# First loads by halves and quarters, constants behind the third unit, repeated bias tiles computed once, last norm spread over three engines

## What is computed

```python
def first_block(...):
    for layer in range(2):
        xn = rmsnorm(h, norm_mix[layer])
        # layer 0: q,k,v,p = xn @ ev_w_in; attention + causal pooling; @ ev_w_out
        # layer 1: gated projections, spatial gating, gated delta rule; @ od_w_out
        h = h + mix
        h = h + memory_cross_attention(rmsnorm(h, ...), mem_n, ...)
        h = h + conv_ffn(rmsnorm(h, ...), ...)
    return rmsnorm(h, final_norm)

def second_block(x, ..., rel_bias, norm_final_g):
    for i in range(2):
        # retention + nsa(...) from rms_norm(x) @ w_in[i], then a gated FFN
    return rms_norm(x, norm_final_g)
```

## Time and profile before

| | us |
|---|---|
| median of 3 runs | 2070.64 (2070.33 to 2073.42) |
| profiled execution, its own time | 2071.59 |
| its span, first to last instruction | 2069.7 |
| PE busy | 2012.6 (97%) |
| POOL busy | 1619.6 (78%) |
| ACT busy | 1085.4 (52%) |
| DVE busy | 866.5 (42%) |

### The profile page before, as it was taken

The page is one execution under the profiler, slowest core; times in us unless marked ns, Lnnn a source line. Parts: engine busy times, 40 slices in busy tenths (PEclk is TensorE's granted clock), DMA queues, the critical chain, the costliest instruction groups (busy, mean ns, idle before and its releaser), DMA issues.

```text
span 2069.7 us, 32431 instructions
## 1 busy us (share of the span) xinstructions
PE 2012.6 (97%) x12426; PEld 1754.1 (85%) x12426; DVE 866.5 (42%) x2030; ACT 1085.4 (52%) x2116; POOL 1619.6 (78%) x1291
## 2 busy tenths in 40 slices
PE   8999999999999999999999989999999999999997
PEld 7788999897888899898778858888997788678886
DVE  3422466066541466173323172563332412644641
ACT  3454566466245566445454585544444554865543
POOL 6495898977286798999799608899997897268997
PEclk9999999999999999999999999999999999999999
DMA  8653555553054476465446604555554467135553
GB/s 301 123 183 123 168 194 169 183 182 120 1 163 163 143 244 215 164 203 185 141 164 191 222 21 163 184 184 191 176 194 151 145 204 227 63 122 176 192 183 112
DMA packets 243470, 343.13 MB, mean 166 GB/s; under 512 B 8787, under 2 KB 171699, under 8 KB 243189
## 3 DMA queue, kind: packets, MB, share of 16 engines
q1 hardware_dynamic: 231320, 331.35, 48.7%
q10 hardware_dynamic: 11997, 9.72, 2.4%
HBM read 336.85 MB, written 4.19 MB: 165 GB/s over the span
## 4 chain that ended last, share of the span: by engine, by line
PE 83%; POOL 6%; DVE 3%; issue 3%; ACT 2%; DMA 1%; POOLq 1%; DVEq 0%; SPq 0%; ACTq 0%
PE bank L757 9%; PE bank L760 9%; PE bank L764 9%; PE bank L779 7%; PE bank L807 7%; PE bank L813 7%; PE bank L810 6%; POOL w_lo L1526 6%; PE bank L837 5%; PE bank L840 5%; PE bank L844 5%; PE bank L784 4%; DVE E L2197 1%; DVE E L2211 1%; DMA ring<-in_w_in 1%
## 5 line engine op out<-in xcount | busy, mean ns | idle before, releaser
L1526 POOL TENSOR_TENSOR w_lo<-ring,w_hi 128x512 fp32r<-128x512 f32 (+1 forms) x1216 | 1575.2, 1314 | 396.8 <-ACT w_hi L1617 359.7
L1617 ACT ACTIVATE w_hi<-ring 128x512 fp32r<-128x512 f32 (+1 forms) x1216 | 757.6, 630 | 791.0 <-PE bank L807 271.3
L757 PE MATMUL bank<-x_pair,w_hi 128*128 128x256 f32 x1504 | 381.6, 286 | 3.0 <-DVE x_pair L2112 2.3
L760 PE MATMUL bank<-x_pair,w_hi 128*128 128x256 f32 x1504 | 379.0, 284 | 0.0
L807 PE MATMUL bank<-w_hi,x_pair 128*128 128x512 f32 (+1 forms) x752 | 299.0, 398 | 2.9 <-issue 1.6
L757 PEld LDWEIGHTS bank<-x_pair,w_hi 128*128 128x128 f32 x1504 | 290.2, 193 | 5.9 <-ACT w_hi L1617 2.7
L810 PE MATMUL bank<-w_hi,x_pair 128*128 128x512 f32 (+1 forms) x752 | 292.9, 390 | 0.0
L760 PEld LDWEIGHTS bank<-x_pair,w_hi 128*128 128x128 f32 x1504 | 290.3, 193 | 0.4
L764 PE MATMUL bank<-x_pair,w_lo 128*128 128x256 f32 x1504 | 242.5, 284 | 0.0
L813 PE MATMUL bank<-w_lo,x_pair 128*128 128x512 f32 (+1 forms) x752 | 234.8, 394 | 4.2 <-POOL w_lo L1526 3.4
L764 PEld LDWEIGHTS bank<-x_pair,w_lo 128*128 128x128 f32 x1504 | 208.3, 193 | 0.0
(11 more groups left out here) (314 smaller groups left out, 2428.6 us busy)
## 6 DMA issues: line engine op xcount, KB each, us to landing
ring<-in_w_in SPq DMA_DIRECT2D x74, 1024.0 KB, 5.1
ring<-in_ffn_w_up SPq DMA_DIRECT2D x44, 1024.0 KB, 5.1
ring<-in_w_ffn_in SPq DMA_DIRECT2D x44, 1024.0 KB, 5.1
ring<-in_ffn_w_down SPq DMA_DIRECT2D x20, 1024.0 KB, 5.0
ring<-in_w_ffn_out SPq DMA_DIRECT2D x20, 1024.0 KB, 5.0
ring<-in_xattn_wkv SPq DMA_DIRECT2D x16, 1024.0 KB, 5.2
ring<-in_w_o_ret SPq DMA_DIRECT2D x16, 1024.0 KB, 5.0
ring<-in_od_w_in SPq DMA_DIRECT2D x12, 1024.0 KB, 5.1
```

What stands on the lines that cost most here:

```text
L757: m = mm(out_, view(w_hi)[:, k, :], x_hi[:, 4 * kh + k, :], start=start, stop=False)
L760: mm(out_, view(w_hi)[:, k, :], x_lo[:, 4 * kh + k, :], start=False, stop=False)
L1526: tt(view(w_lo), src, view(w_hi), ALU.subtract).then_inc(w_lo_ready, 1)
L1617: return A(o, i_, ACT.Copy, **kw)
```

## The change

Seven things, in the order of the program.

1. x is loaded as two halves by channels (`x_loads`, `x_second`), and the first half of eq as two quarters by columns (pieces 0 and 1, then 2 and 3). SP's order is now ident, x half 0, quarter 0, quarter 1, x half 1, eq half 1, ek, memory input, ev half 0, the tables, ev half 1, 16 constants, ep.
2. ACT issues one row load (norm_mix) ahead of its first work; the other 15 go between the rounding of ek's pieces, two behind each. The vector rows are transposed in the middle of ev, and DVE copies them out behind ek.
3. PE begins with 10 matmuls of zeros (`WARM`), 128x512, which wait for a DVE memset alone.
4. `cmpbias`: a bias depends on 128t - 16n only, so the tile (1, n+8) equals (0, n); PE makes 15 tiles, ACT copies 7 of them twice, and DVE fills the masked 8 with -1e30.
5. ACT loads the last gain ahead of the units `3down`.
6. In the last norm DVE takes statistics of columns 0 to 511 before it adds the second half; ACT squares and sums columns 512 to 1023; POOL multiplies columns 0 to 511 by the gain.
7. Once rstd is there, DVE finishes and SP stores columns 512 to 1023, ACT finishes and stores columns 0 to 511.

```diff
+CMP_SEEN = (P - CMP_LEN) // CMP_STRIDE + 1
+CMP_SHIFT = P // CMP_STRIDE
+CMP_TILES = [(0, n) for n in range(CMP_SEEN)] + [(1, n) for n in range(CMP_SHIFT)]
...
+        first_loads = units[0][1][0]
+        (whole_half, whole_source), = first_loads
+        first_weights, first_source = whole_half(0)[:, :, 0:2 * P], whole_source[:, :, 0:2 * P]
+        first_loads[0] = (lambda s: whole_half(s)[:, :, 2 * P:4 * P], whole_source[:, :, 2 * P:4 * P])
...
+            pe.wait_ge(nothing_ready, 1)
+            for _ in range(WARM):
+                mm(bank[0][:, :], nothing[:, 0:P], nothing[:, P:P + PIECE], start=True, stop=True)
             pe.wait_ge(ident_loaded, 16)
-            pe.wait_ge(first_rows, 48)
+            pe.wait_ge(first_rows, 16)
...
+            def turn_x():
+                pe.wait_ge(x_second, 16)
+                turn_h("0m", 1)
...
-            channel_major("eq", x_parts, key="0m", second_half=lambda: turn_h("0m", 1), before_last=turn_rows)
+            channel_major("eq", x_parts, key="0m", second_half=turn_x)
...
-            token_major("ev", x_parts)
+            token_major("ev", x_parts, after=turn_rows)
...
-            for t in range(TT):
-                for n in range(N_CMP):
+            for c, (t, n) in enumerate(CMP_TILES):
...
-            sp.dma_start(h[:, :, :], I["x"][0].rearrange("(t p) n -> p t n", p=P)).then_inc(x_loads, 16)
+            sp.dma_start(h[:, :, 0:512], x_src[:, :, 0:512]).then_inc(x_loads, 16)
+            sp.dma_start(first_weights, first_source).then_inc(first_quarter, 16)
...
             for n, (name, halves) in enumerate(units):
-                if n == 1:
+                if n == RING:
                     sp.dma_start(i_mem, ...).then_inc(mem_loads, 16)
-                if n == RING:
+                if n == RING + 1:
                     load_constants()
                 for j, loads in enumerate(halves):
+                    if n == 0 and j == 1:
+                        sp.dma_start(h[:, :, 512:D], x_src[:, :, 512:D]).then_inc(x_second, 16)
+                    if n == RING and j == 1:
+                        load_table()
...
+            pool.wait_ge(gain_loads, 32)
+            for t in range(TT):
+                B.wait_emptied(pool, ("3down", t, 0))
+                tt(xs[:, t, 0:512], h[:, t, 0:512], gain_row[:, 0:512], ALU.mult).then_inc(gained, 1)
             reciprocal_rms("out")
...
-            round_weights("ek")
+            for p in range(PIECES):
+                round_weights("ek", p, p + 1)
+                for dst, src in later_rows[2 * p:2 * p + 2]:
+                    act.dma_start(dst, src).then_inc(row_loads, 16)
...
+            for t in range(TT):
+                B.wait_emptied(act, ("3down", t, 1))
+                m = A(E[:, t, :], h[:, t, 512:D], ACT.Square, scale=D ** -0.5, accum_out=ms2[:, t:t + 1])
+            m.then_inc(final_square, 1)
+            act.wait_ge(gained, TT)
+            act.wait_ge(rstd_ready, RMS.index("out") + 1)
+            for t in range(TT):
+                copy(xs[:, t, 0:512], xs[:, t, 0:512], scale=rstd[:, t:t + 1]).then_inc(out_done, 1)
...
+                add_last(0)
+                for t in range(TT):
+                    nc.vector.bn_stats(h_stats[:, t, :], h[:, t, 0:512])
+                add_last(1)
+                for t in range(TT):
+                    nc.vector.bn_aggr(h_mv[:, t, :], h_stats[:, t:t + 1, :])
+                drain()
+                tt(ms[:, :], h_mv[:, :, 0], h_mv[:, :, 0], ALU.mult)
+                drain()
+                tt(ms[:, :], ms[:, :], h_mv[:, :, 1], ALU.add)
+                drain()
+                ts(ms[:, :], ms[:, :], 0.5, EPS, ALU.mult, ALU.add)
+                drain()
+                dve.wait_ge(final_square, 1)
+                tt(ms[:, :], ms[:, :], ms2[:, :], ALU.add).then_inc(ms_ready, 1)
...
-            dve.wait_ge(ident_loaded, 16)
+            nc.vector.memset(nothing[:, :].bitcast(F32), 0.0).then_inc(nothing_ready, 1)
+            nc.vector.memset(cmpbias[:, 0, CMP_SEEN:N_CMP, :].rearrange("p b c -> p (b c)"), -FAR)
```

More of the change, by code:

```diff
@@ L152 @@
 N_ROWS_PAD = -(-N_ROWS // P) * P
+EARLY_ROWS = ROWS["norm_mix"][1]
+assert ROWS["norm_mix"][0] == 0 and N_ROWS <= 512
 class Banks:
@@ L384, in build @@
         first_rows = sem("first_rows")
+        nothing_ready = sem("nothing_ready")
+        first_quarter = sem("first_quarter")
+        final_square = sem("final_square")
+        out_done = sem("out_done")
+        gained = sem("gained")
+        x_second = sem("x_second")
         row_loads = sem("row_loads")
@@ L1000, in turn_rows @@
                 B.take(pe, ("vec", 1), 2)
-                for r in range(1, N_ROWS_PAD // P):
+                for r in range(N_ROWS_PAD // P):
                     n = min(P, N_ROWS - r * P)
-                    m = tr(bank[2][:, (r - 1) * P:(r - 1) * P + n], i_rows[0:n, r, :], ident[0:n, 0:n])
+                    m = tr(bank[2][:, r * P:r * P + n], i_rows[0:n, r, :], ident[0:n, 0:n])
                 m.then_inc(full[2], 1)
@@ L1491, in _ @@
                         sp.dma_start(dst(n % RING), src).then_inc(landed[n % RING][j], 16)
[L1492 to L1495, removed]
+            for t in range(TT):
+                sp.wait_ge(h_done, t + 1)
+                sp.dma_start(out[0][t * P:(t + 1) * P, 512:D], xs[:, t, 512:D]).then_inc(stored, 16)
             sp.wait_ge(stored, 64)
@@ L1625, in round_weights @@
                 for p in range(first, end or pieces(name)):
-                    fresh = [j for j in halves_of(name, p) if j not in known]
-                    wait_landed(act, name, fresh)
-                    known.update(fresh)
+                    if name == "eq" and p < 2:
+                        act.wait_ge(first_quarter, 16)
+                    else:
+                        fresh = [j for j in halves_of(name, p) if j not in known]
+                        wait_landed(act, name, fresh)
+                        known.update(fresh)
                     if first_piece[name] or p >= HELD:
@@ L1720, in evacuate, with row_loads_of @@
                 A(dst, src, f, **kw).then_inc(empty[b], 1)
[L1723 to L1726, removed]
+            def row_loads_of(name):
+                r0, count = ROWS[name]
+                src, done = vector_rows(I[name]), 0
                 while done < count:
@@ L1729, in _ @@
                     k = min(count - done, P - r % P)
-                    act.dma_start(i_rows[r % P:r % P + k, r // P, :], src[done:done + k, :]).then_inc(first_rows if r < P else row_loads, 16)
-                    n += r >= P
+                    yield i_rows[r % P:r % P + k, r // P, :], src[done:done + k, :]
                     done += k
-            assert n == ROW_LOADS, n
+            later_rows = [load for name in ROWS if name != "norm_mix" for load in row_loads_of(name)]
+            assert len(later_rows) == ROW_LOADS
+            (dst, src), = row_loads_of("norm_mix")
+            act.dma_start(dst, src).then_inc(first_rows, 16)
             act.wait_ge(ident_loaded, 16)
@@ L2164, in finish, with add_last @@
             def finish():
-                for n in range(2):
+                dve.wait_ge(gain_loads, 32)
+                halves_ = [np.s_[:, t, n * 512:(n + 1) * 512] for n in range(2) for t in range(TT)]
+                def add_last(n):
                     for t in range(TT):
@@ L2252, in evacuate_scaled @@
                 stt(dst, bank[b][:, :].rearrange("p (a b) -> p a b", a=2), scale, two(R_b[:, :]), ALU.mult, ALU.mult).then_inc(empty[b], 1)
[L2254 to L2256 removed]
+            nc.vector.tensor_copy(vecs[:, 0:EARLY_ROWS], bank[3][:, 0:EARLY_ROWS]).then_inc(empty[3], 1)
             drain()
```

57 lines of the change are left out of this document (33 added, 24 removed).

## The result

The changed kernel takes 2062.15 us (median of 6 runs, 2059.13 to 2063.64) where the kernel before took 2073.34 in the same rounds (6 runs, 2070.33 to 2075.84): a ratio of 0.9945, 95% interval 0.9934 to 0.9956, or 11.4 us less. The forecast was 2056.7, in a range that ended at 2061.0. The direction was right and the time missed by 5.4 us. That of the kernel before over 48 runs is 2073.2; one further run of it, 2465.92 us at a granted clock of 0.756, is left out. The gain is 12.6 us on these, against 13.9 in the sum.

What follows compares the result with a forecast made beforehand. PE, busy 97% of the span, was taken as the bound. Terms 3.5 + 1.2 - 0.1 + 6.8 + 2.5 = 13.9 us took the profiled 2071.6 to 2057.7; the median, 0.95 lower, was forecast at 2056.7, range 2053.5 to 2061.0.

Steps and rivals of the forecast that it cites:

- Everything between runs as it did and moves with PE: Between the start, middle and end that the diff touches, the program was taken to run unchanged and shift with PE.
- the tiles' term: Bias tiles ahead of ep: 5.65 for 30 passes saved, 2.8 for ep's lower level, less 1.7 for a fall: 6.8 us.
- Loads 3.5: Start: the first quarter of eq lands at about 6.5, so PE's first matmul stands at 8.15, 3.5 us sooner.
- rival A: Start: small loads do not overlap, the quarter lands no earlier than 8.5, 2 us less gain, 2058.7; chance 0.12.
- Zeros 1.2: Start: with matmuls of zeros, eq's pieces 0 and 1 run at the higher clock, 1.2 us less; ends 0 and 1.6.
- rival C: Start: the matmuls of zeros do nothing for the clock, 2057.9; chance 0.08.
- ACT is not late: Start: ACT, with one load to issue and its table load inside the wait, does not delay the first rounding.
- Moved steps: Row loads in ek, row transposes in ev, later constants: all free except one transpose more, 0.1 us lost.
- rival D: ek: ACT's row loads are held up; at 2.3 us per issue PE loses 25 us, 2082; chance 0.03.
- so I take the fall, with its short length: Bias tiles: the clock still falls, but for 3.4 us as in `2vv`, costing 1.7 us.
- Rival B: Bias tiles: the clock falls and stays low as long as before, 3.3 us less gain, 2060.0; chance 0.12.
- End: Last norm and stores: rstd at 2062.0 instead of 2064.45, first store 2.5 us sooner; ends 1.5 and 3.2.

Runs made afterwards that it cites:

- experiment 3: The changed kernel without the 10 matmuls of zeros (WARM = 0): 2062.11 us over 5 runs, ratio 0.994 to the kernel before.
- experiments 5: The changed kernel with x in one load and the first half of eq in one, as before: 2065.19 us, one run.
- experiment 6: The changed kernel with all 16 of ACT's row loads issued ahead of its first rounding, as before: 2062.72 us, one run.
- experiment 1: The changed kernel, unaltered, timed and profiled again: 2058.44 us over 5 runs, ratio 0.9927 to the kernel before.
- experiment 12: The changed kernel with POOL held until DVE has scaled x, before the remainders of ev: 2061.67 us, one run.

## Why the prediction missed

**The base.** The forecast is 5.4 us under the measured 2062.15, and that has three parts. The sum started from three runs of median 2070.64, and over 48 runs the kernel before has 2073.2: 2.6. The gain was forecast at 13.9 and is 12.6: 1.3. In its first set of runs the kernel after fell 1.6 above the median of its 16 runs (numbers rounded). So two steps of the prediction failed. The first took three runs as the base and held everything else fixed ("Everything between runs as it did and moves with PE"), where the body alone takes between 1979.7 and 1984.25 us by how long the clock is low in it. The second is the size of the tiles' term, below. Apart from the reason that I gave for the length of the fall, the mechanisms of the terms held.

**Start.** Loads 3.5: by the first matmul 3.2 to 3.4. The landing was forecast at 6.5 and is 6.49 to 6.79, the curve and the lag right, and the rival A (8.5) fell. By the Trainium skill's fit for transfers that GpSimd issues ("DMA: Bandwidth & Descriptors", section "Anatomy of one DMA — SWDGE (gpsimd) path"), an estimate, it would be near 8.5 for loads that wait for each other; the trace has 6.79, so here they overlapped, and the measurement decides. Zeros 1.2: 2.0 by experiment 3, and the rival C fell. Between the zeros and the first matmul stand 9 transposes, one opening matmul and a wait of 1.17 us, and the matmuls then run at 0.28 each. So the Trainium skill's rule that transposes do not count for the clock ("TensorE: Matmul & The Clock Gate", Part 4) took nothing away here, and by a wait this short it wasn't put to the test; with waits of 3.05 and 4.31 us (experiments 5 and 6) the lower level came back. With 3.05 the first four matmuls still ran at the higher pace, and the clock fell at 11.9, 1.2 us behind the first. The terms of the loads and the zeros do not add up: without the zeros only 2.3 us of the loads' 3.2 are left at the memory's transposes, since pieces 0 and 1 then take 6.75 us at the lower level (8.42 to 15.17) where before had 6.03. The loads were taken too large and the zeros too small. That the whole start was forecast at 4.6 and is 4.2 to 5.1 is in part luck. "ACT is not late" was right only because its row loads moved too (experiment 6).

**Moved steps.** All free, as worked out: ACT's issues in ek took 0.26 to 0.94 us each and PE's pieces stayed at 1.44 (rival D fell); SP was done with the constants at 35.0 and ep was issued from 35.08, 4.6 us later than the forecast 30.5, and nothing waited for it.

**Tiles.** The term that was mis-sized: 6.8 against 5.7 by the times. Where the low clock lasted 3.4 us, as forecast, the part is 6.5 us shorter; where it lasted 6.8, it is 4.9 to 5.0. The failing step is "so I take the fall, with its short length". The code behind the block is the same in all these traces, so how dense the work there is, from which I argued by one place of one trace, doesn't set the length; that varies from run to run between 3.4 and 6.8 us, with 10.2 once. What sets it stays open. Rival B was wrong as a fixed length too, and half right as a warning.

**End.** 2.5: 2.4 in the trace, 2.1 in the times. rstd starts 1.37 us behind DVE's last add and is there 0.70 later (2.1 forecast), ACT's second sum ends at 2055.22, in time for DVE's last step at 2055.57; no table is loaded for the squares, and the stores keep their length: each step as forecast.

**The range.** It took in the rivals but neither the spread of the base (three runs) nor that of the low clock in the body, which by experiment 1 is 3.4 us between two executions of one program. With the base alone, 2.6 higher, it would have reached about 2064.

## What to carry to other kernels

Before a small gain is forecast, find what varies between executions of one program (here the length of the low-clock stretches behind blocks of small matmuls), and compare traces part by part between marks: a part that the diff doesn't touch took back 3.65 us by chance. Take the base from as many runs as the gain needs: three were 2.6 us off. A block of cheap work may cover another engine's chain, so look for who would be late before it is dissolved. Where two engines end a wait within 0.3 us of each other, the gain belongs to both edits and to neither alone.

## What the hardware showed

Between PE's first and last matmul the low clock comes in stretches of 3.4, 6.8 or 10.2 us and of no other length, in all 14 traces. Two executions of one program can differ by 13.6 us at the low clock (experiment 1), and that goes with 5 us of time.

Six 16-column matmuls cost 1.0 us among 128x512 ones and 0.7 in a block of their own at full clock (3.52 / 30 x 6).

The clock column doesn't show PE's pace until the first change: in experiment 3 it shows 1.00 from 12 to 13 us with 7 matmuls of 128x256 in 1 us, in experiment 6 0.50 with the same 7 from 14 to 15, and 11 once it shows 1.00 again. First of experiment 3, then of 6:

```profile
12.00:13.00 1.00, 1.00 (x7) 1.00 (x7) 0.00 (x0) 0.52 (x1) 0.48 (x1) 1.00 1.10 348
```

```profile
14.00:15.00 1.00, 1.00 (x7) 1.00 (x7) 0.00 (x0) 0.00 (x0) 1.00 (x2) 0.50 1.09 345
...
18.00:19.00 1.00, 1.00 (x11) 1.00 (x9) 0.76 (x2) 1.00 (x4) 0.00 (x0) 1.00 1.08 391
```

DVE's scaling of a 128x1024 tile takes 0.7 us alone and 1.8 to 4.3 beside POOL's subtractions (two take 1.42 and 5.98, experiment 12).
